# A hybrid encoder layer in split float32: both weight tiles of an output do their wide products first, then both their narrow ones

## What is computed

```python
proj = x @ w_in[l]
q, k, v, u, g_att, g_ssm = jnp.split(proj, splits, axis=-1)
y_att = _neighbourhood_attention(heads(q), heads(k), heads(v), na_rpb[l]) @ w_na_out[l]
y_s = (y_f + y_b + s5_d[l] * ug)                     # two _s5_scan directions
y_s = gelu(y_s);  y_s = y_s * sigmoid(y_s @ w_glu[l] + b_glu[l])
mix = (g_att * y_att + g_ssm * (y_s @ w_s5_out[l])) @ w_out[l]
h = _layer_norm(DEEPNORM_ALPHA * x + mix, ln1_g[l], ln1_b[l])
ff = (silu(h @ w_ffn_gate[l]) * (h @ w_ffn_up[l])) @ w_ffn_down[l]
x = _layer_norm(DEEPNORM_ALPHA * h + ff, ln2_g[l], ln2_b[l])
```

## Time and profile before

| what | value |
|---|---|
| median of 3 runs | 1420.28 us (1419.93 to 1421.84) |
| profiled execution, its own time | 1420.9 us |
| its span, first to last instruction | 1419.1 us |
| mean granted TensorE clock | 0.997 |
| PE busy | 1404.9 us (99%) |
| DVE busy | 949.6 us (67%) |
| ACT busy | 725.5 us (51%) |
| HBM read | 259.41 MB, 186 GB/s over the span |

### The profile page before, as it was taken

One profiled execution on the slowest core, in us unless ns is written; L12 is line 12 of the kernel. 1 busy time (PEld: TensorE's weight loads), 2 busy tenths in 40 slices (PEclk: granted clock), 3 DMA queues, 4 the chain that ended last, 5 costly groups with the idle time before them and its releaser, 6 DMA issues.

```text
span 1419.1 us, 23454 instructions
## 1 busy us (share of the span) xinstructions
PE 1404.9 (99%) x8984; PEld 1209.6 (85%) x8984; DVE 949.6 (67%) x1312; ACT 725.5 (51%) x1034; POOL 80.8 (6%) x86
## 2 busy tenths in 40 slices
PE   8899999999999999999999999999999999999998
PEld 7788888888888888887888888888888888888886
DVE  7988898889876779756655555655555554545454
ACT  5355655555653885435644544444445443333332
POOL 2800000000000000000022221000000000000001
PEclk9999999999999999999999999999999999999998
DMA  8676555556445667664656566666666656666663
GB/s 289 192 218 183 175 150 178 154 176 180 147 155 156 190 230 263 184 200 134 186 186 191 188 184 190 191 184 189 227 184 189 189 188 196 190 196 194 193 192 104
DMA packets 87840, 265.62 MB, mean 187 GB/s; under 512 B 13778, under 2 KB 22098, under 8 KB 87380
## 3 DMA queue, kind: packets, MB, share of 16 engines
q1 hardware_dynamic: 84228, 261.19, 59.6%
q10 hardware_dynamic: 3536, 3.38, 0.7%
HBM read 259.41 MB, written 5.11 MB: 186 GB/s over the span
## 4 chain that ended last, share of the span: by engine, by line
PE 96%; DVE 2%; ACT 0%; DMA 0%; issue 0%; SPq 0%; ACTq 0%; DVEq 0%
PE bank L1553 41%; PE bank L1555 21%; PE bank L1567 9%; PE bank L1569 9%; PE bank L1568 9%; PE bank L1642 2%; PE bank L1611 1%; PE bank L1663 1%; DVE wlo L922 1%; PE bank L1624 1%; PE bank L1843 1%; PE bank L1673 0%; PE bank L1689 0%; DMA raw<-wstream 0%; DVE scratch L945 0%; PE bank L1655 0%
## 5 line engine op out<-in xcount | busy, mean ns | idle before, releaser
L922 DVE TENSOR_TENSOR wlo<-raw,whi 128x1024 fp32r<-128x1024 f32 x463 | 567.9, 1227 | 338.0 <-ACT whi L495 333.9
L495 ACT ACTIVATE whi<-raw 128x1024 fp32r<-128x1024 f32 x463 | 490.2, 1059 | 461.6 <-PE bank L1555 247.4
L1553 PE MATMUL bank<-act,whi 128*128 128x512 f32 x2304 | 585.5, 396 | 5.9 <-DVE wlo L922 3.6
L1553 PEld LDWEIGHTS bank<-act,whi 128*128 128x128 f32 x2304 | 413.8, 189 | 84.2 <-DVE wlo L922 4.8
L1555 PEld LDWEIGHTS bank<-act,wlo 128*128 128x128 f32 x2304 | 314.3, 190 | 22.7
L1555 PE MATMUL bank<-act,wlo 128*128 128x256 f32 x2304 | 321.2, 282 | 0.0
L1567 PE MATMUL bank<-whi,mid 128*128 128x512 f32 x352 | 136.9, 389 | 0.0
L1568 PE MATMUL bank<-wlo,mid 128*128 128x512 f32 x352 | 136.9, 389 | 0.0
L1569 PE MATMUL bank<-whi,mid 128*128 128x512 f32 x352 | 136.9, 389 | 0.0
L1568 PEld LDWEIGHTS bank<-wlo,mid 128*128 128x128 f32 x352 | 66.1, 188 | 13.8
L1567 PEld LDWEIGHTS bank<-whi,mid 128*128 128x128 f32 x352 | 66.1, 188 | 13.7
(11 more groups left out here) (176 smaller groups left out, 1165.6 us busy)
## 6 DMA issues: line engine op xcount, KB each, us to landing
raw<-wstream SPq DMA_DIRECT2D x463, 512.0 KB, 3.7
lnrow<-lnrows SPq DMA_DIRECT2D x3, 1024.0 KB, 6.4
xraw<-xT SPq DMA_DIRECT2D x8, 256.0 KB, 6.2
bcn<-bc_rows SPq DMA_DIRECT2D x8, 256.0 KB, 3.7
bm<-bias SPq DMA_DIRECT2D x8, 256.0 KB, 4.0
tb<-lag_dram SPq DMA_DIRECT2D x32, 64.0 KB, 3.5
hp<-xtok SPq DMA_DIRECT2D x4, 512.0 KB, 4.7
out<-hp SPq DMA_DIRECT2D x8, 256.0 KB, 2.6
```

The lines of the kernel that those rows point to most:

```text
L495: act.activation(whi[:, c % SPL, :], raw[:, c % RAW, :], ACT.Copy).then_inc(hi_ready, 1)
L922: dve.tensor_tensor(wlo[:, c % SPL, :], raw[:, c % RAW, :], whi[:, c % SPL, :].bitcast(F32), ALU.subtract).then_inc(lo_ready, 1)
L1553: pe.matmul(bank[:, :], whi[:, s, i * P:(i + 1) * P], both, start=start and i == 0, stop=stop and i == kn - 1)
```

## The change

In the head loop and in the `Fori` part and tail of the feed-forward, the two tiles of an output no longer run one after the other. The first tile of the pair does only its 8 products of 512 columns. With the second tile come its own 8 products of 512, then the first tile's 8 products of 256, then its own 8 of 256. Both tiles count `w_used` at their last product of 256, so the first tile's slot is given back after the second one's wide products. In the head loop what stood behind the first tile (for example `s5_in` at 0) now stands between the two runs of wide products. All other stages, and the first 12 tiles of the feed-forward, keep the old order.

```diff
-            def prod_w(m, c, act, k0, kn, bank, start, stop, ready=None):
+            def prod_hi(m, c, act, k0, kn, bank, start, stop, ready=None):
...
+                    pe.matmul(bank[:, :], whi[:, c % SPL, i * P:(i + 1) * P], both, start=start and i == 0,
+                              stop=stop and i == kn - 1, skip_group_check=True)
+
+            def prod_lo(m, c, act, k0, kn, bank, stop):
+
                 for i in range(kn):
-                    mm = pe.matmul(bank[:, 0:T], wlo[:, s, i * P:(i + 1) * P], act[:, k0 + i, 0, :], start=False,
+                    mm = pe.matmul(bank[:, 0:T], wlo[:, c % SPL, i * P:(i + 1) * P], act[:, k0 + i, 0, :], start=False,
                                    stop=stop and i == kn - 1, skip_group_check=True)
                 mm.then_inc(w_used, 1)
+
+            def prod_w(m, c, act, k0, kn, bank, start, stop, ready=None):
+
+                prod_hi(m, c, act, k0, kn, bank, start, stop, ready)
+                prod_lo(m, c, act, k0, kn, bank, stop)
+
+            def prod_half(m, c, act, h, bank):
+
+                prod_hi(m, c, act, 8 * h, 8, bank, h == 0, h == 1)
+                if h == 1:
+                    prod_lo(m, c - 1, act, 0, 8, bank, False)
+                    prod_lo(m, c, act, 8, 8, bank, True)
...
-                    prod_w(0, c, act16, 8 * (j % 2), 8, ps[bank_of(n)], j % 2 == 0, j % 2 == 1)
+                    prod_half(0, c, act16, j % 2, ps[bank_of(n)])
...
-                        prod_w(m, H_FF + 4 * i + q, act16, 8 * (q % 2), 8, ps[bank_of(n)], q % 2 == 0, q % 2 == 1)
+                        prod_half(m, H_FF + 4 * i + q, act16, q % 2, ps[bank_of(n)])
```

More of the change, by code:

```diff
@@ L1544, in wait_split @@
                 pe.wait_ge(lo_ready, 12 * m + (c + 1))
-            def prod_w(m, c, act, k0, kn, bank, start, stop, ready=None):
-                s = c % SPL
+            def prod_hi(m, c, act, k0, kn, bank, start, stop, ready=None):
                 for i in range(kn):
@@ L1552, in prod_w @@
                     both = act[:, k0 + i, :, :].rearrange("p h n -> p (h n)")
-                    pe.matmul(bank[:, :], whi[:, s, i * P:(i + 1) * P], both, start=start and i == 0, stop=stop and i == kn - 1)
+                    pe.matmul(bank[:, :], whi[:, c % SPL, i * P:(i + 1) * P], both, start=start and i == 0,
+                              stop=stop and i == kn - 1, skip_group_check=True)
+            def prod_lo(m, c, act, k0, kn, bank, stop):
                 for i in range(kn):
-                    mm = pe.matmul(bank[:, 0:T], wlo[:, s, i * P:(i + 1) * P], act[:, k0 + i, 0, :], start=False,
+                    mm = pe.matmul(bank[:, 0:T], wlo[:, c % SPL, i * P:(i + 1) * P], act[:, k0 + i, 0, :], start=False,
                                    stop=stop and i == kn - 1, skip_group_check=True)
                 mm.then_inc(w_used, 1)
+            def prod_w(m, c, act, k0, kn, bank, start, stop, ready=None):
[6 more added lines that the diff above has]
+                    prod_lo(m, c, act, 8, 8, bank, True)
             def prod_b(c, act, k0, banks, start, stop, rows_apart=False):
```

## The result

The changed kernel takes 1427.8 us (median of 4 runs, 1426.2 to 1428.72) against 1420.71 of the kernel before on the same chip: ratio 1.0043, 95% interval 1.003 to 1.0055, that is 4.3 to 7.8 us longer. The forecast was 1425.9 us with a range of 1424 to 1428.5. The profiled execution took 1426.2 us, with a span of 1424.4 instead of 1419.1.

What follows compares the result with a forecast made beforehand. TensorE, busy 99% of the span, was taken as the bound. Stands of 4.0 + 1.2 + 1.6 = 6.8, taken as 7.0, less 1.4 for switches, gave +5.6 on 1420.28: 1425.9 us, range 1424 to 1428.5.

Steps and rivals of the forecast that it cites:

- What bounds: Whole kernel: TensorE is busy 99% of the span, so time saved or new waits in both changed loops count one to one.
- The switches: Fewer wide-narrow switches save 0.017 us a pair: 1.4 us over 82 feed-forward pairs, 0.0 in the head loop.
- the rival that order gains nothing: Both loops: no gain at the switches, same stands, 1427.3 us; chance 0.17.
- Heads 1 to 6: Head loop: tile 0's later release delays VectorE's chain, so tile 5 is late by 0.67 us a head, 4.0 in six.
- Heads 0 and 7: First and last head: tile 5 is late by 1.2 us in head 0 and 1.6 in head 7.
- The feed-forward's room: Feed-forward: a pair takes 5.57 us; the next pair's second tile is in time by 0.11 us, costing nothing.
- The waits on record: Sign in TensorE's waits: eight new waits for VectorE's `wlo`, 0.6 to 1.6 us each, always at tile 5 of a head.
- What else moves: Other tiles, ScalarE's copies and table evacuations, the row decay, DMAs and banks: later in places, but none late.
- 7.0: Head loop: total stands at tile 5, 4.0 + 1.2 + 1.6 = 6.8 us, taken as 7.0 with roundings.

Runs made afterwards that it cites:

- the feed-forward alone: The new order in the feed-forward only, the head loop keeping the old one: 1419.73 us against 1421.68 of the kernel before, ratio 0.999.
- two orders with the same number of switches: Old head loop; feed-forward pairs wide-wide-narrow-narrow (1419.73 us, ratio 0.999) or wide-narrow-narrow-wide (1419.57 us, ratio 0.9984), against the kernel before.

## Why the prediction was right

*What bounds.* TensorE was the bound and each stand went into the time, as said: its busy time didn't move, and the stages sum to 5.85 us, within the interval of the loss.

*The switches.* Forecast 1.4 us of gain, measured 1.45 in the changed kernel and 1.64 with the feed-forward alone. Confirmed by two orders with the same number of switches, against the rival that order gains nothing.

*Heads 1 to 6.* Forecast 0.67 each, at tile 5; measured 0.64, at tile 5. The place and size were right, the cause was named too narrowly: the late release of tile 0 was taken to start VectorE's chain, and the release of tile 10 of the head before, which holds tile 1, whose subtraction "at about 0" the prediction had worked out too, starts an unbroken chain that ends 0.05 us earlier. Neither alone gives the time back.

*Heads 0 and 7.* Forecast 1.2 and 1.6, measured 1.16 and 1.52.

*The feed-forward's room.* Forecast 0.11 us and no stand; no pair waited, and the slot given back 0.96 us later made a pair 6.43, as the same sum gave it. The terms of the new pair as written, 1.84 + 1.81 + 0.95 + 0.96, make 5.56 and not 5.57; measured are 5.567.

*The waits on record.* They were to be 0.6 to 1.6 us each. In heads 1 to 6 the row says less, 0.39 in head 3, for the reason in the last section.

*What else moves.* This step failed at one place: nothing was to be late but tile 5, and the third tile of the attention output stood 0.8 us. After head 7, ScalarE's copy of the second attention-output tile waits for tile 10 of head 7, and behind that copy stand on ScalarE the gelu (with a table load), the copy of the third tile and the copy of the last gate output, whose bank the third tile takes. VectorE subtracts the third tile, and only then adds from that bank. The timelines after:

```profile
469.31 1.06 ACT L495 ACTIVATE whi<-raw 128x1024 fp32r<-128x1024 f32 x1 [2.20 <-PE bank L1558]
470.39 1.28 ACT L730 ACT_TABLE_LOAD   x1
471.68 2.01 ACT L730 ACTIVATE u<-u 128x1024 f32<-128x1024 f32 x2
473.59 1.04 ACT L495 ACTIVATE whi<-raw 128x1024 fp32r<-128x1024 f32 x1
474.54 0.36 ACT L654 ACTIVATE gs<-bank 128x256 f32<-128x256 f32 x1
...
474.67 1.23 DVE L922 TENSOR_TENSOR wlo<-raw,whi 128x1024 fp32r<-128x1024 f32 x1 [3.04 <-ACT whi L495]
...
475.81 0.42 DVE L1260 TENSOR_TENSOR gs<-bank,gs 128x256 f32<-128x256 f32 x1
476.28 1.69 PEld L1552 LDWEIGHTS bank<-act8a,whi 128*128 128x128 f32 x8 [0.73 <-DVE gs L1260]
```

The third tile was due at 472.80 + 2.79 = 475.59. Its own subtraction ends only at 475.90 and the add at 476.23, so the bank came last but was not alone. The stand vanished with tiles 10-11 in the old order. I had walked one head round and not the seam behind the last one. That the sum came out near is luck in part: this +0.80 met a head loop of +6.50 where 7.0 was taken. Forecast +5.6, +5.85 by the stages, 7.1 between the medians with an interval of 4.3 to 7.8, which holds both.

## What to carry to other kernels

When a slot is given back later, don't stop at its own reader: follow every in-order queue from each changed release, round the loop and over its ends, and look for a second chain that arrives at the same point; undoing one cause of two that are tied gives almost nothing back (0.05 and 0.02 us of 0.64 a head here), and that doesn't clear it. Before you pay for a cheaper order with a later release, look for an order with the same number of switches that gives the slots back as before: turning every second tile round gained as much as the change did in its good part. And where a stage has one in-order engine near full, moving work behind an urgent instruction there can be worth as much as moving the release: it brought heads 1 to 6 from 45.64 back to 44.97 here.

## What the runs showed that was not expected

The wait on record understates a stand: at tile 5 TensorE's row says 0.39 us idle where the head got 0.64 longer, since the recorded end of the transposes ahead of it (0.60 us for four that start 0.11 apart) reaches into the stand. The weight load's row for the same place says 0.62:

```profile
261.83 0.30 PEld L1552 LDWEIGHTS bank<-act,whi 128*128 128x128 f32 x2 [0.62 <-DVE wlo L922]
```
